# The last expert iteration of each layer, ordered by request instead of by pair of experts

## The reference, cut to what matters

```python
def hierarchical_moe(h, ...):
    ...
    hid = jax.nn.silu(jnp.einsum('bsd,edf->bsef', h, w_gate)) * jnp.einsum('bsd,edf->bsef', h, w_up)
    hid = hid * combine[..., None].astype(h.dtype)
    return jnp.einsum('bsef,efd->bsd', hid, w_down)
...
    for l in range(DEPTH):
        ...
        y = hierarchical_moe(modulate(xp, sh2, sc2), *moe_w)
        xp = layer_norm(DEEPNORM_ALPHA * xp + g2 * y, ln2_g[l], ln2_b[l])
```

## Time and profile before

| | us |
|---|---|
| median of three runs | 1079.57 |
| lowest and highest | 1078.3, 1082.82 |
| the profiled execution's own time | 1075.45 |
| its span | 1073.4 |
| PE busy in the span | 970.0 |

### The profile page before, as it was taken

The page is one execution under the profiler, slowest core; times in us unless marked ns, Lnnn a source line. Parts: engine busy times, 40 slices in busy tenths (PEclk is TensorE's granted clock), DMA queues, the critical chain, the costliest instruction groups (busy, mean ns, idle before and its releaser), DMA issues.

```text
span 1073.4 us, 15615 instructions
## 1 busy us (share of the span) xinstructions
PE 970.0 (90%) x6820; PEld 597.3 (56%) x6820; DVE 323.7 (30%) x744; ACT 226.6 (21%) x469; POOL 26.4 (2%) x50
## 2 busy tenths in 40 slices
PE   3999899998999999979959998999999999997893
PEld 1888758776743434324338886687884343432531
DVE  2121323222751312112171132331266222211116
ACT  2102314300141312112121132241014221211111
POOL 0200000010000000000010000000000000000000
PEclk9999999999999999999979999999999999999897
DMA  9939854596629999999894216765462999999960
GB/s 380 410 151 358 334 225 157 208 327 259 266 107 430 417 427 430 427 429 428 323 426 174 106 38 258 314 273 207 177 250 90 425 428 430 430 427 428 422 259 39
DMA packets 38525, 324.59 MB, mean 302 GB/s; under 512 B 4920, under 2 KB 5048, under 8 KB 9392
## 3 DMA queue, kind: packets, MB, share of 16 engines
q1 hardware_dynamic: 34816, 313.02, 71.2%
q0 software_dynamic: 3200, 9.09, 2.5%
q10 hardware_dynamic: 432, 1.39, 0.3%
HBM read 321.05 MB, written 2.42 MB: 301 GB/s over the span
## 4 chain that ended last, share of the span: by engine, by line
PE 82%; DVE 6%; DMA 5%; ACT 3%; issue 3%; SPq 0%; DVEq 0%; ACTq 0%
PE ps L797 17%; PE ps L846 10%; PE ps L692 9%; PE ps L718 6%; PE ps L987 5%; PE ps L901 5%; PE ps L973 5%; PE ps L750 5%; PE ps L621 3%; PE ps L810 3%; DMA expert_gate_up<-in_w_gu 2%; PE ps L856 2%; PE ps L642 2%; DMA dense<-in_w_ada 2%; PE ps L938 2%
## 5 line engine op out<-in xcount | busy, mean ns | idle before, releaser
L797 PE MATMUL ps<-expert_gate_up,gathered_prompt 128*32 128x512 f32 x896 | 197.3, 593 | 5.4 <-ACT gathered_sample L1167 2.3
L797 PE MATMUL ps<-expert_gate_up,gathered_sample 128*32 128x512 f32 x896 | 197.2, 593 | 0.0
L797 PEld LDWEIGHTS ps<-expert_gate_up,gathered_prompt 128*32 128x32 f32 x896 | 56.3, 110 | 132.7 <-issue 129.7
L846 PE MATMUL ps<-expert_down,hiddenT 128*32 128x512 f32 x1024 | 115.9, 595 | 10.2 <-ACT hiddenT L1187 4.7
L692 PE MATMUL ps<-hT,dense 128*128 128x256 f32 x512 | 115.9, 385 | 0.0
L692 PEld LDWEIGHTS ps<-hT,dense 128*128 128x128 f32 x512 | 97.6, 193 | 15.6 <-issue 2.5
L1575 DVE SCALAR_TENSOR_TENSOR y_lo<-ps,slot_weight,y_hi 128x512 fp32r<-128x512 f32 x64 | 48.1, 751 | 101.1 <-ACT y_hi L1199 101.1
L846 PEld LDWEIGHTS ps<-expert_down,hiddenT 128*32 128x32 f32 x1024 | 31.3, 109 | 81.4 <-issue 54.1
L1558 DVE TENSOR_TENSOR hidden<-hidden,ps 128x256 f32<-128x256 f32 x32 | 13.5, 421 | 194.2 <-ACT hidden L1183 194.2
L718 PE MATMUL ps<-dense,hT 128*128 128x256 f32 (+1 forms) x320 | 66.7, 372 | 1.8 <-ACT hT L1124 1.8
L621 PE MATMUL ps<-dense,cond 128*32 128x256 f32 x768 | 51.4, 395 | 16.7 <-ACT cond L1221 12.0
(11 more groups left out here) (212 smaller groups left out, 986.0 us busy)
## 6 DMA issues: line engine op xcount, KB each, us to landing
expert_gate_up<-in_w_gu SPq DMA_DIRECT2D x64, 2048.0 KB, 19.3
expert_down<-in_w_dn SPq DMA_DIRECT2D x64, 1024.0 KB, 14.2
dense<-in_w_ada SPq DMA_DIRECT2D x48, 1024.0 KB, 9.2
dense<-in_w_in SPq DMA_DIRECT2D x28, 1024.0 KB, 11.9
dense<-in_w_o SPq DMA_DIRECT2D x8, 1024.0 KB, 6.6
dense<-in_w_out SPq DMA_DIRECT2D x8, 1024.0 KB, 4.8
dense<-in_w_c SPq DMA_DIRECT2D x4, 1024.0 KB, 24.4
dense<-in_w_uq SPq DMA_DIRECT2D x4, 576.0 KB, 6.5
```

The source lines that it names most:

```text
L797: last = mm(ps[r0:r0 + 32, q, :], xg[s][:, k, at_:at_ + CAP], w_gu[BUFFER[i * EPI + 2 * q + j]][:, k, :], start=(k == 0), stop=(k == KD - ...
L846: last = mm(ps[32 * e:32 * e + 32, banks[c], :], h, w_dn[BUFFER[i * EPI + e]][:, f, c * 512:(c + 1) * 512], start=(f == 0), stop=(f == 1), ...
```

## The change

In iteration 7, of both layers, PE works by request. All of request 0's gate/up comes first; request 1's comes in four pieces of two steps, and between the pieces stand request 0's transposes, its down product and its scatter, and the scatters of iteration 6. Request 1's transposes, down product and scatter come last. DVE's and ACT's programs follow: request 0's whole tail now stands on DVE before request 1's last two `low`, and ACT's square root for request 0 before request 1's `high`. Since both of the last two gate/up counts now cover all four experts, `expert_pass` gives the later count for experts 28 and 29.

```diff
@@ expert_pass @@
-            return 2 * i + 2 if i == 0 else 2 * i + (e % EPI) // 2 + 1
+            return 2 * i + 2 if i in (0, ITERS - 1) else 2 * i + (e % EPI) // 2 + 1
@@ tensor @@
                 pe.wait_ge(*reached(m, "selT_copied", i + 2))
-                for q in range(2):
-                    gate_up_pair(m, None, i, q)
-                    scatter(m, i - 1, i - 1, q, False)
-                turn_pairs(m, i)
-                down(m, None, i, i, 0, (2, 3), True, i + 2)
-                down(m, None, i, i, 1, (2, 3), True, i + 2, (0,))
+                gate_up_request(m, i, 0, 0, range(0, 8))
+                scatter(m, i - 1, i - 1, 0, False)
+                gate_up_request(m, i, 1, 1, range(0, 2))
+                turn_request(m, i, 0, 0)
+                gate_up_request(m, i, 1, 1, range(2, 4))
+                pe.wait_ge(*reached(m, "lo_done", 4 * i))
+                down(m, None, i, i, 0, (2, 3), False, ITERS + 1)
+                gate_up_request(m, i, 1, 1, range(4, 6))
                 scatter(m, i, i, 0, False)
-                down(m, None, i, i, 1, (2, 3), True, i + 2, (1,))
+                gate_up_request(m, i, 1, 1, range(6, 8))
+                scatter(m, i - 1, i - 1, 1, False)
+                turn_request(m, i, 1, 1)
+                down(m, None, i, i, 1, (2, 3), False, ITERS + 2)
                 scatter(m, i, i, 1, False)
@@ scalar @@
-                for q in range(2):
-                    silu(m, i, q, q)
-                turned_pairs(m, i + 2)
-                for s in range(2):
-                    for c in range(2):
-                        high(m, i, i, s, c, 2 + c, i + 2)
+                silu(m, i, 0, 0)
+                turned_request(m, 0, 0, ITERS + 1)
+                for c in range(2):
+                    high(m, i, i, 0, c, 2 + c, i + 2)
+                silu(m, i, 1, 1)
+                turned_request(m, 1, 1, ITERS + 2)
                 sqrt(8, 9)
+                for c in range(2):
+                    high(m, i, i, 1, c, 2 + c, i + 2)
@@ vector: moe_sum @@
-                dve.wait_ge(*reached(M[l], "sc_filled", 2 * (ITERS - 1) + s + 1))
+                dve.wait_ge(*reached(M[l], "sc_filled", 2 * ITERS - 2 if s == 0 else 2 * ITERS))
@@ vector @@
-                for q in range(2):
-                    hidden_product(m, i, q, q)
+                hidden_product(m, i, 0, 0)
                 for c in range(2):
                     low(m, i, i, 0, c, 2 + c)
-                low(m, i, i, 1, 0, 2)
                 moe_sum(l, 0)
-                low(m, i, i, 1, 1, 3)
                 moe_residual(l, 0)
+                hidden_product(m, i, 1, 1)
                 e = row_sums(y_sum, 0, 8, LN_EPS)
                 centre(y_sum, ln2, 0)
                 scale(e, ln2, 0, 8, x2_ready, l)
+                low(m, i, i, 1, 0, 2)
                 more = l + 1 < DEPTH
                 if more:
                     e = row_sums(x, 0, 10, LN_EPS)
+                low(m, i, i, 1, 1, 3)
+                if more:
                     prepare(e, 0, 10)
                 moe_sum(l, 1)
```

More of the change, by code:

```diff
@@ L313, in build @@
                      "h_filled": 2 * ITERS, "silu_done": 2 * ITERS, "hid_done": 2 * ITERS,
-                     "hidT_filled": ITERS + 1, "hidT_copied": ITERS + 1, "y_filled": 4 * ITERS,
+                     "hidT_filled": ITERS + 2, "hidT_copied": ITERS + 2, "y_filled": 4 * ITERS,
                      "hi_done": 4 * ITERS, "lo_done": 4 * ITERS, "sc_filled": 2 * ITERS}
```

## The result

| us | before | changed |
|---|---|---|
| median (lowest to highest) | 1078.93 (1078.3 to 1082.82, 4 runs) | 1064.59 (1061.37 to 1069.14, 4 runs) |
| profiled execution, its span | 1075.45, 1073.4 | 1061.37, 1059.3 |

The ratio is 0.9868, with a 95% interval of 0.9844 to 0.9892: 14.3 us faster in the medians, 14.1 in the profiled executions. 10.4 was forecast. The changed kernel's four runs include its profiled execution, those of the kernel before do not.

The account below looks back on a forecast made before the run. The prediction took DVE to bound both ends of the expert phase. Terms of -4.5 (layer 1) and -5.9 (layer 0) gave -10.4 us: 1069.2 us on the median of the runs, range 1064.5 to 1074.8.

Parts of the forecast that it names:

- the likeliest case: The summed gain holds, -10.4 us to 1069.2, with its own range of 1066 to 1072; chance 0.74.
- The bound: Both ends of the expert phase, in layers 0 and 1, are bound by DVE, not by PE.
- The iteration on PE: Iteration 7, reordered by request, costs PE about 0.25 us more in each layer.
- The new wait: In iteration 7, PE's transposes wait for request 1's hidden product, behind request 0's sum and residual on DVE; costs 0.2 us.
- Term 1: Layer 1's end: request 1's sum starts 28.65 us into iteration 7 instead of 33.16; -4.5 us.
- Term 2: Layer 0's end: the negated mean is ready at 29.7 us into iteration 7 instead of 35.56; -5.9 us.
- The clock: Between the layers, cost left as it is; -3.1 us if it did not fall, +2.2 if low twice as long in `project`.
- The loads: Layer 1's dense weight loads, issued later during layer 0's iteration 7, stay hidden; cost 0, over 14 us of cover.
- The gate/up weights: Slower rival: PE stalls at iteration 7's start for experts 30 and 31, up to +16, 1085 us; chance 0.04.
- The late root: Rival: request 0's square root on ACT holds DVE 0.7 us in both layers, -9.0, 1070.6 us; chance 0.10.

Follow-up runs that it names:

- e4: The changed kernel with PE's new order, but request 0's residual and LayerNorm on DVE and root on ACT put back late; ratio 1.0 to the kernel before, median 1078.86 us.
- e7: The changed kernel with request 0's transposes straight after scatter(6,0), gate/up pieces regrouped and DVE's statistics earlier; median 1063.63 us, ratio 0.985 to the kernel before.
- e2: The kernel before with the new order on all three engines in layer 1 only; median 1074.55 us, ratio 0.995.
- e3: The kernel before with the new order on all three engines in layer 0 only; median 1071.51 us, ratio 0.9931.
- e5: The kernel before with 22 unused extra matmuls in PE's gap between the layers; median 1074.13 us, ratio 0.9955.
- e1: The changed kernel timed again, nothing altered; median 1065.33 us, ratio 0.9866 to the kernel before.
- e10: The changed kernel with all loads of layer 1's dense weights held until layer 0's last down product is done; median 1064.11 us, ratio 0.9868 to the kernel before.

## Why the prediction was right, and where its size was off

The mechanism was right: each of the two ends got shorter by about its term. The size was short: 10.4 forecast, 14.3 measured in the medians and 14.1 in the profiled execution, where the clock alone is 3.0 of the 3.7 that were missing. The measured 1064.59 lies 0.1 us inside the lower end of the range given (1064.5), and below the 1066 to 1072 of the likeliest case; that it is still inside is luck, with runs from 1061.37 to 1069.14.

- **The bound**: DVE at both ends of the expert phase. Shown by e4 (PE's order without DVE's: 1.0) against the changed kernel.
- **The iteration on PE.** Forecast: request 0's scatter ends at 18.5, DVE's sum starts at 18.6, PE's last down product starts at 22.55. Measured in layer 0: 18.35, 18.37, and in layer 1 22.39 (1043.23 - 1020.84). The seam of 0.05 that I added is 0.1 for the first two pieces (1.85) and none for the third (1.72); the down product took 3.43 and not 3.6. The 3.43 is counted to the start of the next piece; the 3.6 was the length of a row, which reaches to the end of its last matmul, and that row is 3.62 in the changed kernel, too.
- **The new wait.** Forecast: request 1's hidden product behind the residual costs PE 0.2. It was there, and e7, which takes it away, finds 0.21 for it.
- **Term 1**, -4.5: measured -4.71 (28.45 against 33.16), and -4.72 in e2.
- **Term 2**, -5.9: measured -6.51 at the start of the transposes (30.38 against 36.89). The negated mean was ready at 29.05, not 29.7: 0.23 is the earlier start of the sum, some 0.2 the operations from the statistics of x on, which took 2.69 (543.15 to 545.84) where I had 2.9, and the rest lies in between.
- **The clock**: this is the term of the sum that was mis-sized, put at nothing. "I leave the cost as it is" held for none of the profiles of the changed kernel and e3: where the clock stayed up (the changed kernel's first profile) transposes and projection were 0.87 + 2.13 = 3.0 shorter than before, close to the -3.1 given as the bound, and e5 shows the same 3.0 with the clock alone. In e1 and e3 the clock fell later: the way from the transposes to the projection was 0.55 and 0.66 shorter than before, and the projection gained nothing. In the first profile the parts are -4.71 - 6.51 - 3.0 = -14.2, for the -14.1 of the spans. That they meet so closely is luck in part: iteration 7 of layer 0 starts 0.6 later than before, and the way from `qk` to iteration 7 of layer 1 is 0.5 shorter.
- **The loads**: cost 0, by e10. **The gate/up weights**: no wait of PE for them; the slower rival did not come.
- **The late root**: it did not come in the changed kernel, where the root was ready at 540.53 and wanted at 540.96, a cover of 0.43 where 0.6 was forecast. In e7 DVE came sooner, and it did come, with 1.33. The Trainium skill ("ScalarE: Activation LUTs", "What ACT_TABLE_LOAD costs") puts a drain of 1.38 us to each switch; the rows agree on the load's 1.28, but in the changed kernel and in e7 it starts 0.02 behind the copy ahead of it, and the root 0.02 or less behind its end. So here the switch costs 1.3 us, and the measurement decides.

Still open: how often the clock stays up at the boundary, and what decides it. It did in one of three profiles of kernels with the changed order of layer 0 as it stands (the changed kernel, e1, e3), and in e10, which differs only in loads; in e7 it was low for 3.4 us. With PE's long gap (before, e2, e4) it was low for 13.7 us each time.

## What to carry to other kernels

Where two independent streams end in a long tail on a slow engine, finish one stream's matmuls early, and let the other's run beside its tail; here reordering the matmuls paid only with the tail's engine reordered too. An engine's queue then has to be read instruction by instruction: here a table load and a root, harmless before, had 0.43 us of cover left, and one step further they were the limit. A gap of TensorE that gets shorter can be worth more than its length, since what follows it may run at the higher clock (0 to 6.8 us of low clock here, where the long gap had 13.7); count both cases. And a single profile can show either case: compare the same stretch in several before a difference is put down to a change.

## What I had not expected of the hardware

The same program took either clock at the same place: none of the boundary low in one execution, 6.8 us of it in another (13.7 before the change). Behind one and the same wait of 2.3 us in layer 1, the clock fell in six of twelve profiles, which cost some 1.5 us in five of them and 3.1 in e1. And a gap that was filled with unused matmuls, 22 of them in 9.8 us, made the boundary 3.0 us shorter without moving the start of the transposes. Part of the spread of the executions was made before iteration 7 of layer 0, where all these kernels are alike: its start varies from 516.2 to 520.9 us, with a mean clock of 0.94 to 0.99 up to 30 us and of 0.89 to 0.98 from 30 to 60 us.
